# Nine of eleven feed-forward chunks: gate and up products with the weights held in the array and the tokens moving

## The chip, the cores and the metric

The kernel runs on one core of a Trainium2 chip. The metric is the device time of one launch in microseconds (us); lower is better. The core has a matrix engine (TensorE, PE in the profile, its weight loads under PEld), VectorE (DVE), ScalarE (ACT), GpSimd (POOL) and SyncE (SP), which issues the loads from the chip's memory (HBM). The engines run side by side and meet only at semaphores.

## The reference, cut to what matters

Two blocks run over 256 tokens of width 1024. The first holds four feed-forward layers (two for each of its two mixer layers), the second ends in a mixture of experts. What the change touches is the feed-forward layer, four times:

```python
def rmsnorm(x, g):
    y = x * rsqrt(mean(x * x, axis=-1) + 1e-6)      # one factor for each token
    return y * g                                    # one factor for each column
def swiglu(h, w_gate, w_up, w_down):                # 1024 -> 2816 -> 1024
    return (silu(h @ w_gate) * (h @ w_up)) @ w_down
x = x + 0.5 * swiglu(rmsnorm(x, norm), w_gate, w_up, w_down)
```

## The kernel before, in words

Weights come as pieces of 128x2048 fp32 values through a ring of three buffers. Each piece is rounded by ScalarE to the matrix engine's one-pass format (`high`, `round_piece`, L230), and VectorE takes the rest (`low = raw - high`, `split_piece`, L236). A product is then three matmuls (`product`, L241): high x high, high x low and low x high, accumulated in PSUM. Each of the three has a weight load of its own.

The hidden width of 2816 is cut into 11 chunks of 256. For a chunk there are two pieces with gate and up columns (`gate_up_parts`, each with 4 of the 8 row blocks of 128) and one piece with the rows of the down matrix. The transposed tokens `hT_high`, `hT_low` are not yet multiplied by the root factor of the norm (`rstd`); that factor is one number for each token and is applied afterwards.

`gate_up_pe` (L510) holds 128x128 of the tokens in the array and moves 512 weight columns, 256 of gate and 256 of up. The result of tile `tt` has the tokens in its partitions and stands in PSUM bank `GU[tt]`. ScalarE reads the gate half (`gate_act`, Silu with `scale=rstd`), VectorE multiplies the up half by `rstd` and by the gate (`gate_dve`), and the result `act_tok` has the tokens in its partitions. The down product needs it the other way round: `act_turn_pe` (L522) makes four 128x128 transposes into `TURN_A`, ScalarE rounds them to `aT_high` (`inner`, L635) and VectorE takes the rest into `aT_low` (L673). `down_tile` holds 128x128 of these and moves 512 columns of the down piece.

The order on the matrix engine in `ffn_pe`, for `chunk(c, m)`: first half of the gate and up products of chunk m+1 (24 matmuls), the transposes of chunk m, the second half of chunk m+1 (24), the down products of chunk m (24). `chunk(0, 0)` stands alone, eight more turns are a loop (`pe.Fori(0, N_CHUNKS - 3)`), and the last two chunks are written out, since they are woven with the start of the next norm. ScalarE and VectorE have loops of the same length with their own order: round/split of a piece, the gate work, round/split, `inner`, round/split. Each layer so has 11 sets of transposes, one for each chunk.

Names and lines to follow: `used` counts the pieces that the matrix engine is done with, `gu_first` the first bank of a chunk's gate and up products, `act_ready` the finished `act_tok` tiles, `a_low` the finished `aT_low`, `split` the pieces ready to be multiplied.

Of the kernel before, what the change touches and what calls it, by code (L numbers as in the profile page):

```python
# [28 lines left out]
F32 = mybir.dt.float32  # L29
# [7 lines left out]
P = 128  # L37
# [57 lines left out]
def build(nc, t, out):  # L95
    ctx = ExitStack()
    with ctx:
        def sb(name, shape, dt=F32):
            return ctx.enter_context(nc.sbuf_tensor(name, shape, dt))

        def sem(name):
            return ctx.enter_context(nc.semaphore(name))
# [15 lines left out]
        gate = sb("gate", [P, TT, CHUNK])  # L118
        act_tok = sb("act_tok", [P, TT, CHUNK])
# [64 lines left out]
        a_turned, a_high, a_low = sem("a_turned"), sem("a_high"), sem("a_low")  # L184
        in_first, in_copied = sem("in_first"), [sem("in_copied0"), sem("in_copied1")]
# [26 lines left out]
        def scales_with(r, n):  # L212

            return 0 if isinstance(r, int) and r == 0 else r * n
# [333 lines left out]
        AS = N_CHUNKS + 1  # L548

        def ffn_pe(pe, i, k, k_next):  # L550
# [37 lines left out]
            for tt in range(TT):  # L588
                pe.wait_ge(act_ready, 2 * (m + done) + tt + 1)
                gate_up_pe(pe, at + 2, 0, tt)  # L590
            act_turn_pe(pe, 2 * (m + done + 1))
# [5 lines left out]
            act_turn_pe(pe, 2 * (m + done + 2), (0,))  # L597
# [8 lines left out]
            act_turn_pe(pe, 2 * (m + done + 2), (1,))  # L606
# [23 lines left out]
        def ffn_act(act, i, k, k_next, aside=lambda: None):  # L630
# [10 lines left out]
            def chunk(p, r, number, a_number, gu_used):  # L641
                round_piece(act, p, r)
                gate_act(act, 0, gu_first, number)
                gate_act(act, 1, used, gu_used)
                round_piece(act, p + 1, r)
                inner(a_number)
                round_piece(act, p + 2, r)

            have_rstd(act, k)
            chunk(b + 2, 0, done + 1, a_done + 1, b + 2)  # L650
            with act.Fori(0, N_CHUNKS - 3) as c:
                chunk(b + 5, c, c + (done + 2), c + (a_done + 2), c * 3 + (b + 4))
            aside()
            m = N_CHUNKS - 2
            at = b + 3 * m
            round_piece(act, at + 2)
            gate_act(act, 0, gu_first, done + m + 1)
            gate_act(act, 1, used, at + 1)
            round_piece(act, at + 3)
            round_piece(act, at + 4)  # L660
            inner(a_done + m + 1)
            round_piece(act, at + 5)
            gate_act(act, 0, gu_first, done + m + 2)
            inner_of(0, a_done + m + 2)
            gate_act(act, 1, used, at + 4)
            tail_act(act, k_next, at + 6, at + 7, lambda: inner_of(1, a_done + m + 3))

        def ffn_dve(dve, i, k, k_next, aside=lambda: None):
# [11 lines left out]
            def chunk(p, r, number, a_number):  # L680
                split_piece(dve, p, r)
                for tt in range(TT):
                    gate_dve(dve, number * 2, tt)
                split_piece(dve, p + 1, r)
                inner(a_number)
                split_piece(dve, p + 2, r)

            have_rstd(dve, k)
            chunk(b + 2, 0, done + 1, a_done + 1)
            with dve.Fori(0, N_CHUNKS - 3) as c:  # L690
                chunk(b + 5, c, c + (done + 2), c + (a_done + 2))
            aside()
            m = N_CHUNKS - 2
            at = b + 3 * m
            split_piece(dve, at + 2)
            for tt in range(TT):
                gate_dve(dve, (done + m + 1) * 2, tt)
            split_piece(dve, at + 3)
            split_piece(dve, at + 4)
            inner(a_done + m + 1)  # L700
            gate_dve(dve, (done + m + 2) * 2, 0)
            split_piece(dve, at + 5)
            inner_of(0, a_done + m + 2)
            gate_dve(dve, (done + m + 2) * 2, 1)
            tail_dve(dve, k_next, at + 6, at + 7, 0.5, lambda: inner_of(1, a_done + m + 3))
# [1621 lines left out]
```

## Time and profile before

| | value |
|---|---|
| median of 3 runs | 1688.84 us (1688.37 to 1692.07) |
| profiled execution | 1687.54 us, its span 1685.5 us |
| PE busy | 1466.4 us, 87% of the span |
| PEld busy | 1124.0 us, 67% |
| DVE busy | 751.7 us, 45% |
| ACT busy | 615.4 us, 37% |
| mean granted TensorE clock | 0.938 of full |

The span is the time from the first to the last instruction of the profiled execution; some 2 us lie around it. "Busy" of PE counts overlapped matmuls once. A view with groups of instructions gives the mean length of one; since matmuls are pipelined, the length of one (0.39 us) is more than the distance from one start to the next (0.23 us), and only the distance tells what one costs in a stream.

### The profile page before, as it was taken

What the parts mean: (1) busy time and instruction counts of PE and PEld (TensorE: products, weight loads), DVE (VectorE), ACT (ScalarE), POOL (GpSimd) and SP (SyncE); (2) the same over time, 40 slices, a digit from 0 to 9 for tenths busy, and PEclk for the clock granted to TensorE, in tenths of its full rate; (3) what the DMA queues carried; (4) which work ended last, traced back from release to release, by engine and by line L of the source; (5) the groups of instructions that cost most, each with busy time, mean ns of one, the idle gap of its engine ahead of it and who ended that gap; (6) DMA issues with size and microseconds to landing.
All of it is one profiled execution on the core that took longest, in us unless ns stands there. A gap on an engine that the chain in (4) does not pass through costs nothing.

```text
span 1685.5 us, 22438 instructions
## 1 busy us (share of the span) xinstructions
PE 1466.4 (87%) x8732; PEld 1124.0 (67%) x8732; DVE 751.7 (45%) x985; ACT 615.4 (37%) x783; POOL 34.3 (2%) x66
## 2 busy tenths in 40 slices
PE   7999998699999999999999999966587666766766
PEld 5888887588888888877788887855554434424434
DVE  4454648755455545465454546645521120221121
ACT  5343545354434534466553445643210110111010
POOL 4000000000000000000010000010000000000000
PEclk9999989899999999999999999987797888888978
DMA  7646544035555555553365554542599999999997
GB/s 215 218 158 216 184 166 175 1 125 201 173 202 172 184 191 185 206 164 118 125 199 180 197 176 153 197 124 102 212 418 418 418 417 417 418 419 418 418 417 315
DMA packets 172620, 396.56 MB, mean 235 GB/s; under 512 B 11361, under 2 KB 109745, under 8 KB 156192
## 3 DMA queue, kind: packets, MB, share of 16 engines
q1 hardware_dynamic: 169152, 392.20, 62.4%
q0 software_dynamic: 3296, 3.73, 1.1%
q8 instruction: 28, 0.46, 0.1%
q14 instruction: 16, 0.13, 0.0%
q10 hardware_dynamic: 128, 0.03, 0.0%
HBM read 393.83 MB, written 1.05 MB: 234 GB/s over the span
## 4 chain that ended last, share of the span: by engine, by line
PE 67%; DMA 12%; SPq 9%; DVE 7%; ACT 2%; issue 2%; POOL 0%; DVEq 0%; ACTq 0%
PE psum L243 19%; PE psum L245 18%; PE psum L244 18%; DMA pair_ring<-in_w_exp_up 9%; SPq L1945 8%; PE psum L1990 4%; PE psum L2011 2%; DMA scratch<-proj 2%; PE psum L2030 1%; DMA pair_ring<-in_w_exp_down 1%; DVE low L238 1%; PE psum L525 1%; DVE hT_low L408 1%; ACT hT_high L398 1%; PE psum L1161 1%
## 5 line engine op out<-in xcount | busy, mean ns | idle before, releaser
L238 DVE TENSOR_TENSOR low<-raw,high 128x2048 fp32r<-128x2048 f32 x179 | 406.5, 2289 | 138.7 <-ACT high L234 135.8
L243 PE MATMUL psum<-high,hT_high 128*128 128x512 f32 x1088 | 437.1, 402 | 13.9 <-DVE low L2258 5.0
L245 PE MATMUL psum<-high,hT_low 128*128 128x512 f32 x1088 | 427.9, 393 | 0.0
L244 PE MATMUL psum<-low,hT_high 128*128 128x512 f32 x1088 | 427.2, 393 | 0.0
L234 ACT ACTIVATE high<-raw 128x2048 fp32r<-128x2048 f32 x179 | 338.2, 1911 | 61.9 <-PE psum L245 53.9
L243 PEld LDWEIGHTS psum<-high,hT_high 128*128 128x128 f32 x1088 | 206.7, 190 | 59.8 <-issue 9.5
L245 PEld LDWEIGHTS psum<-high,hT_low 128*128 128x128 f32 x1088 | 206.2, 190 | 44.7
L244 PEld LDWEIGHTS psum<-low,hT_high 128*128 128x128 f32 x1088 | 207.1, 190 | 40.8
L2011 PE MATMUL psum<-pair_ring,scratch 128*32 128x256 f32 x2048 | 144.8, 435 | 55.4 <-DMA pair_ring<-in_w_exp_up 54.3
L2011 PEld LDWEIGHTS psum<-pair_ring,scratch 128*32 128x32 f32 x2048 | 68.5, 122 | 128.2 <-DMA pair_ring<-in_w_exp_up 74.3
L635 ACT ACTIVATE aT_high<-psum 128x512 fp32r<-128x512 f32 x40 | 23.9, 598 | 323.1 <-PE psum L525 323.1
L673 DVE TENSOR_TENSOR aT_low<-psum,aT_high 128x512 fp32r<-128x512 f32 x40 | 27.7, 692 | 255.3 <-ACT aT_high L635 255.3
L243 PE MATMUL psum<-high,aT_high 128*128 128x512 f32 x352 | 137.4, 390 | 0.2
L244 PE MATMUL psum<-low,aT_high 128*128 128x512 f32 x352 | 137.0, 389 | 0.0
L245 PE MATMUL psum<-high,aT_low 128*128 128x512 f32 x352 | 137.0, 389 | 0.0
L2030 PE MATMUL psum<-pair_ring,scratch 128*32 128x256 f32 x1024 | 82.4, 476 | 44.7 <-DMA pair_ring<-in_w_exp_down 40.4
L2081 ACT ACTIVATE scratch<-psum 32x256 f32<-32x256 f32 x64 | 23.9, 373 | 199.6 <-PE psum L2030 199.2
L2103 DVE TENSOR_TENSOR scratch<-scratch,psum 128x128 f32<-128x128 f32 x32 | 9.2, 288 | 188.0 <-ACT scratch L2076 188.0
L2030 PEld LDWEIGHTS psum<-pair_ring,scratch 128*32 128x32 f32 x1024 | 40.5, 130 | 72.9 <-issue 53.3
L2076 ACT ACTIVATE scratch<-psum 128x128 f32<-128x128 f32 x32 | 8.9, 278 | 210.3 <-PE psum L2011 210.3
L1990 PE MATMUL psum<-proj,h 128*128 128x128 f32 x288 | 71.1, 409 | 8.2 <-DVE proj L1898 8.2
L1990 PEld LDWEIGHTS psum<-proj,h 128*128 128x128 f32 x288 | 69.4, 335 | 13.1 <-issue 13.1
(317 smaller groups left out, 1172.7 us busy)
## 6 DMA issues: line engine op xcount, KB each, us to landing
pair_ring<-in_w_exp_gate SPq DMA_DIRECT2D x64, 1024.0 KB, 22.1
pair_ring<-in_w_exp_up SPq DMA_DIRECT2D x64, 1024.0 KB, 22.8
pair_ring<-in_w_exp_down SPq DMA_DIRECT2D x64, 1024.0 KB, 22.4
raw<-in_ffn_w_gate SPq DMA_DIRECT2D x88, 512.0 KB, 4.1
raw<-in_ffn_w_up SPq DMA_DIRECT2D x88, 512.0 KB, 5.3
raw<-in_ffn_w_down SPq DMA_DIRECT2D x88, 512.0 KB, 4.0
raw<-in_gla_w_in SPq DMA_DIRECT2D x24, 512.0 KB, 4.6
raw<-in_sb_w_in SPq DMA_DIRECT2D x24, 512.0 KB, 4.6
```

Of the source, the lines that this page charges most:

```text
L234: act.activation(high[:, p % RING, :], raw_of(p), ACT.Copy).then_inc(rounded, 1)
L238: dve.tensor_tensor(low[:, p % RING, :], raw_of(p), high[:, p % RING, :].bitcast(F32), ALU.subtract).then_inc(split, 1)
L243: pe.matmul(psum_out, lhs_high, rhs_high, start=start, stop=False, skip_group_check=True)
L244: pe.matmul(psum_out, lhs_high, rhs_low, start=False, stop=False, skip_group_check=True)
L245: return pe.matmul(psum_out, lhs_low, rhs_high, start=False, stop=stop, skip_group_check=True)
L635: act.activation(flat(aT_high), TURN_A, ACT.Copy).then_inc(a_high, 1)
L673: dve.tensor_tensor(flat(aT_low), TURN_A, flat(aT_high).bitcast(F32), ALU.subtract).then_inc(a_low, 1)
L1945: sp.dma_start(dst, src).then_inc(pair_landed[i % PAIRS], 16)
L1990: ins = pe.matmul(BATCH_X[:, k * P:(k + 1) * P], h[:, tt, :].rearrange("p (n k) -> p k n", k=KD)[:, k, :], picks[:, tt * P:(tt + 1) * P], ...
L2011: ins = pe.matmul(out_rows, batch_x[:, kk, j * SLOTS:(j + 1) * SLOTS], w[:, :, k, c * P:(c + 1) * P], start=kk == 0, stop=kk == KD - 1, sk ...
L2030: ins = pe.matmul(ITEM_Y[q * SLOTS:(q + 1) * SLOTS, :], item_aT[:, c * SLOTS:(c + 1) * SLOTS], w[:, c, q * QUARTER:(q + 1) * QUARTER], sta ...
L2081: ins = act.activation(batch_y[j * SLOTS:(j + 1) * SLOTS, q * QUARTER:(q + 1) * QUARTER], ITEM_Y[q * SLOTS:(q + 1) * SLOTS, :], ACT.Copy)
```

## The change

The gate and up products of chunks 1 to 9 of each layer change their roles. `gate_up_turned_pe` holds 128x128 of the weights in the array (one block `c` of 128 columns of gate, then of up) and moves the 256 tokens. A bank `GU[c]` so holds gate (256 columns) and up (256 columns) of 128 hidden units, with the hidden units in the partitions, as the down product wants them. A piece of half a chunk takes 2 x 4 x 2 x 3 = 48 matmuls of 256 columns in place of 24 of 512. The transposes of these chunks go away.

The root factor now varies along the columns, so a row of it is made once for each layer: two matmuls with `rstd` spread over 128 columns as the held operand and the identity as the moving one (`ROOT_ROWS`), copied to `root_rows`. VectorE multiplies each bank by it (`block_norm`, 128x512), ScalarE makes the Silu (`block_silu_act`), VectorE the product with up (`block_gate`), ScalarE the rounding (`block_high_act`) and VectorE the rest (`block_low`). Chunks 0 and 10 of each layer stay as they were. `aT_high` is written as soon as the down products of the chunk before are done.

```diff
+        def gate_up_turned_pe(pe, q, half, c):
+            for k in range(4):
+                kk = 4 * half + k
+                for i in range(2):
+                    cols = slice(i * CHUNK + c * P, i * CHUNK + (c + 1) * P)
+                    ins = product(pe, GU[c][:, i * TOKENS:(i + 1) * TOKENS], four_k(high, q)[:, k, cols],
+                                  four_k(low, q)[:, k, cols], hT_high[:, kk, :], hT_low[:, kk, :],
+                                  start=kk == 0 and i == 0, stop=kk == KD - 1)
+            if c == 1:
+                ins.then_inc(used, 1)
+            elif half == 1:
+                ins.then_inc(gu_first, 1)
...
             def chunk(c, m, start=False):
...
-                for tt in range(TT):
-                    pe.wait_ge(act_ready, scales_with(c, 2) + (2 * (m + done) + tt + 1))
-                    gate_up_pe(pe, b + at + 2, 0, tt)
-                act_turn_pe(pe, scales_with(c, 2) + 2 * (m + done + 1))
+                for n in range(2):
+                    if m == 0:
+                        pe.wait_ge(act_ready, 4 * i + n + 1)
+                    else:
+                        pe.wait_ge(block_normed, scales_with(c, 2) + (BLOCKS * i + 2 * (m - 1) + n + 1))
+                    gate_up_turned_pe(pe, b + at + 2, 0, n)
+                if m == 0:
+                    act_turn_pe(pe, 4 * i + 2)
+                    have_rstd(pe, k)
+                    for tt in range(TT):
+                        ins = pe.matmul(ROOT_ROWS[:, tt * P:(tt + 1) * P], rstd[:, tt:tt + 1].to_broadcast([P, P]),
+                                        ident[:, :], start=True, stop=True, skip_group_check=True)
+                    ins.then_inc(rows_of_roots, 1)
...
-                for tt in range(TT):
-                    gate_up_pe(pe, b + at + 3, 1, tt)
+                for n in range(2):
+                    gate_up_turned_pe(pe, b + at + 3, 1, n)
...
+            with act.Fori(0, N_CHUNKS - 3) as c:
+                number = c * 2 + (BLOCKS * i + 1)
+                round_piece(act, b + 5, c)
+                for n in range(2):
+                    block_silu_act(n, number)
+                round_piece(act, b + 6, c)
+                act.wait_ge(used, c * 3 + (b + 5))
+                for n in range(2):
+                    block_high_act(n, number)
+                round_piece(act, b + 7, c)
...
+            with dve.Fori(0, N_CHUNKS - 3) as c:
+                number = c * 2 + (BLOCKS * i + 1)
+                split_piece(dve, b + 5, c)
+                block_norm(0, gu_first, c + (done + 2), c + (a_done + 1))
+                block_norm(1, used, c * 3 + (b + 4), None)
+                for n in range(2):
+                    block_gate(n, number)
+                split_piece(dve, b + 6, c)
+                for n in range(2):
+                    block_low(n, number)
+                split_piece(dve, b + 7, c)
```

In the written-out part after the loop the transposes of chunk 9 go, and the wait ahead of the first gate and up products of chunk 10 is on `block_normed`. `gate` and `act_tok` share a new buffer `inner_sb` with the normed banks.

## Rows read from the trace of the kernel before

**Rows 1.** The page: busy time of each engine, and the chain's lines.
```profile
PE 1466.4 (87%) x8732; PEld 1124.0 (67%) x8732; DVE 751.7 (45%) x985; ACT 615.4 (37%) x783; POOL 34.3 (2%) x66
...
PE psum L243 19%; PE psum L245 18%; PE psum L244 18%; DMA pair_ring<-in_w_exp_up 9%; SPq L1945 8%; PE psum L1990 4%; PE psum L2011 2%; DMA scratch<-proj 2%; PE psum L2030 1%; DMA pair_ring<-in_w_exp_down 1%; DVE low L238 1%; PE psum L525 1%; DVE hT_low L408 1%; ACT hT_high L398 1%; PE psum L1161 1%
```
**Rows 2.** Busy time in layers 0 and 2 of four: window, length, engines (count), clock, DMA share, GB/s.
```profile
28.00:190.00 162.00, 162.00 (x728) 133.87 (x727) 80.47 (x61) 67.58 (x61) 5.90 (x9) 0.99 0.57 195
...
541.00:720.00 179.00, 178.64 (x815) 147.44 (x813) 93.40 (x83) 81.61 (x85) 0.00 (x0) 1.00 0.55 188
```
**Rows 3.** Timeline of PE, loop turns: start us, us, line, operation.
```profile
85.15 0.60 PE L525 MATMUL psum<-ident,act_tok 128*128 128x128 f32 x4
...
101.71 0.39 PE L245 MATMUL psum<-high,hT_low 128*128 128x512 f32 x1
101.95 0.60 PE L525 MATMUL psum<-ident,act_tok 128*128 128x128 f32 x4
102.30 0.48 PE L243 MATMUL psum<-high,hT_high 128*128 128x512 f32 x1
102.61 0.40 PE L244 MATMUL psum<-low,hT_high 128*128 128x512 f32 x1
...
104.70 0.39 PE L244 MATMUL psum<-low,hT_high 128*128 128x512 f32 x1
...
105.15 0.39 PE L243 MATMUL psum<-high,hT_high 128*128 128x512 f32 x1
...
118.53 0.39 PE L245 MATMUL psum<-high,hT_low 128*128 128x512 f32 x1
118.76 0.60 PE L525 MATMUL psum<-ident,act_tok 128*128 128x128 f32 x4
```
**Rows 4.** Timeline of PE: 16 moving columns, each with a full weight load.
```profile
216.51 0.26 PE L245 MATMUL psum<-gkw_high,hT_low 128*128 128x16 f32 x1
...
219.19 0.26 PE L245 MATMUL psum<-gkw_high,hT_low 128*128 128x16 f32 x1
```
**Rows 5.** Lengths ns min/median/max: the products with 16 and with 512 moving columns.
```profile
L243 PE MATMUL psum<-gkw_high,hT_high x9: 172/256/256, 216.4 to 219.0; 128*128 128x16 f32 x9
...
L245 PE MATMUL psum<-high,hT_low x3: 388/389/389, 23.8 to 25.1; 128*128 128x512 f32 x3
```
**Rows 6.** Timeline of PE: full fp32 matmuls, 128 and 256 moving columns.
```profile
301.54 2.05 PE L927 MATMUL psum<-scratch 128*128 128x128 f32 x16 [1.41 <-DVE scratch L1053]
...
318.38 2.43 PE L936 MATMUL psum<-proj,scratch 128*128 128x256 f32 x10 [1.38 <-DVE scratch L1089]
320.64 0.59 PE L939 MATMUL psum<-proj,scratch 128*128 128x256 f32 x2
```
**Rows 7.** Timeline of DVE and ACT within one loop turn, and in turn 0.
```profile
103.21 0.69 DVE L673 TENSOR_TENSOR aT_low<-psum,aT_high 128x512 fp32r<-128x512 f32 x1 [7.34 <-ACT aT_high L635]
105.02 4.49 DVE L238 TENSOR_TENSOR low<-raw,high 128x2048 fp32r<-128x2048 f32 x2 [1.11 <-ACT high L234]
109.43 0.87 DVE L618 SCALAR_TENSOR_TENSOR act_tok<-psum,rstd,gate 128x256 f32<-128x256 f32 x2
...
102.58 0.60 ACT L635 ACTIVATE aT_high<-psum 128x512 fp32r<-128x512 f32 x1 [9.04 <-PE psum L525]
103.08 3.71 ACT L234 ACTIVATE high<-raw 128x2048 fp32r<-128x2048 f32 x2
106.69 0.46 ACT L614 ACTIVATE gate<-psum,rstd 128x256 f32<-128x256 f32 x1
...
37.80 4.50 DVE L238 TENSOR_TENSOR low<-raw,high 128x2048 fp32r<-128x2048 f32 x2 [1.11 <-ACT high L234]
```
**Rows 8.** Timeline of PE among the experts: 64 matmuls in one burst.
```profile
1223.60 3.64 PE L2011 MATMUL psum<-pair_ring,scratch 128*32 128x256 f32 x64
```
**Rows 9.** Windows of PE around the 16-column products: length, busy, clock, DMA, GB/s.
```profile
216.40:219.20 2.80, 2.80 (x28) 1.00 0.63 162
219.60:223.60 4.00, 4.00 (x21) 0.50 0.96 359
```

More of the change, by code:

```diff
@@ L117, in build @@
         h = sb("h", [P, TT, D])
-        gate = sb("gate", [P, TT, CHUNK])
-        act_tok = sb("act_tok", [P, TT, CHUNK])
+        inner_sb = sb("inner_sb", [P, 2, 2 * CHUNK])
+        gate, act_tok = (inner_sb[:, i, :].rearrange("p (a n) -> p a n", a=TT) for i in range(2))
         gain = sb("gain", [P, 2, D])
@@ L184, in build @@
         a_turned, a_high, a_low = sem("a_turned"), sem("a_high"), sem("a_low")
+        rows_of_roots, roots_spread = sem("rows_of_roots"), sem("roots_spread")
+        block_normed, block_silu, block_act, block_high = (sem("block_" + n) for n in ("normed", "silu", "act", "high"))
         in_first, in_copied = sem("in_first"), [sem("in_copied0"), sem("in_copied1")]
@@ L596, in ffn_pe @@
             down_tile(pe, at + 4, 0)
-            act_turn_pe(pe, 2 * (m + done + 2), (0,))
+            act_turn_pe(pe, 4 * (i + 1), (0,))
             gate_up_pe(pe, at + 3, 1, 1)
@@ L605, in ffn_pe @@
             down_tile(pe, at + 4, 1)
-            act_turn_pe(pe, 2 * (m + done + 2), (1,))
+            act_turn_pe(pe, 4 * (i + 1), (1,))
             x_turn_pe(pe, k_next, 0)
@@ L639, in inner_of, with block_silu_act, block_high_act @@
                 act.activation(inner_tile(aT_high, tt), turned_inner(tt), ACT.Copy).then_inc(a_high, 1)
[L641 to L647, printed above, removed]
-            have_rstd(act, k)
-            chunk(b + 2, 0, done + 1, a_done + 1, b + 2)
-            with act.Fori(0, N_CHUNKS - 3) as c:
-                chunk(b + 5, c, c + (done + 2), c + (a_done + 2), c * 3 + (b + 4))
+            def block_silu_act(n, number):
+                act.wait_ge(block_normed, number + n)
+                act.activation(inner_sb[:, n, 0:TOKENS], inner_sb[:, n, 0:TOKENS], ACT.Silu).then_inc(block_silu, 1)
+            def block_high_act(n, number):
+                act.wait_ge(block_act, number + n)
+                act.activation(aT_high[:, n, :], inner_sb[:, n, 0:TOKENS], ACT.Copy).then_inc(block_high, 1)
+            have_rstd(act, k)
+            round_piece(act, b + 2)
+            gate_act(act, 0, gu_first, done + 1)
+            gate_act(act, 1, used, b + 2)
+            round_piece(act, b + 3)
+            inner(3 * i + 1)
+            round_piece(act, b + 4)
+            with act.Fori(0, N_CHUNKS - 3) as c:
+                number = c * 2 + (BLOCKS * i + 1)
[7 more added lines that the diff above has]
+                round_piece(act, b + 7, c)
             aside()
@@ L678, in inner_of, with block_norm @@
                                   ALU.subtract).then_inc(a_low, 1)
[L680 to L686, printed above, removed]
-            have_rstd(dve, k)
-            chunk(b + 2, 0, done + 1, a_done + 1)
-            with dve.Fori(0, N_CHUNKS - 3) as c:
-                chunk(b + 5, c, c + (done + 2), c + (a_done + 2))
+            def block_norm(n, counter, value, lows):
+                dve.wait_ge(counter, value)
+                if n == 0:
+                    dve.wait_ge(a_low, lows)
+                dve.tensor_tensor(inner_sb[:, n, :].rearrange("p (o n) -> p o n", o=2),
+                                  GU[n].rearrange("p (o n) -> p o n", o=2),
+                                  root_rows.rearrange("p (o n) -> p o n", o=1).to_broadcast([P, 2, TOKENS]),
+                                  ALU.mult).then_inc(block_normed, 1)
@@ new lines, in ffn_dve @@
+            have_rstd(dve, k)
+            split_piece(dve, b + 2)
+            for tt in range(TT):
+                gate_dve(dve, 4 * i + 2, tt)
+            split_piece(dve, b + 3)
+            inner(3 * i + 1)
+            dve.wait_ge(rows_of_roots, i + 1)
+            dve.tensor_copy(root_rows, ROOT_ROWS).then_inc(roots_spread, 1)
+            split_piece(dve, b + 4)
+            dve.wait_ge(roots_spread, i + 1)
+            with dve.Fori(0, N_CHUNKS - 3) as c:
+                number = c * 2 + (BLOCKS * i + 1)
+                split_piece(dve, b + 5, c)
+                block_norm(0, gu_first, c + (done + 2), c + (a_done + 1))
+                block_norm(1, used, c * 3 + (b + 4), None)
+                for n in range(2):
+                    block_gate(n, number)
+                split_piece(dve, b + 6, c)
+                for n in range(2):
+                    block_low(n, number)
+                split_piece(dve, b + 7, c)
@@ L694, in ffn_dve @@
             at = b + 3 * m
+            number = BLOCKS * (i + 1) - 1
             split_piece(dve, at + 2)
-            for tt in range(TT):
-                gate_dve(dve, (done + m + 1) * 2, tt)
+            block_norm(0, gu_first, done + m + 1, a_done + m)
+            block_norm(1, used, at + 1, None)
+            for n in range(2):
+                block_gate(n, number)
             split_piece(dve, at + 3)
+            for n in range(2):
+                block_low(n, number)
             split_piece(dve, at + 4)
-            inner(a_done + m + 1)
-            gate_dve(dve, (done + m + 2) * 2, 0)
+            gate_dve(dve, 4 * i + 4, 0)
             split_piece(dve, at + 5)
-            inner_of(0, a_done + m + 2)
-            gate_dve(dve, (done + m + 2) * 2, 1)
-            tail_dve(dve, k_next, at + 6, at + 7, 0.5, lambda: inner_of(1, a_done + m + 3))
+            inner_of(0, 3 * i + 2)
+            gate_dve(dve, 4 * i + 4, 1)
+            tail_dve(dve, k_next, at + 6, at + 7, 0.5, lambda: inner_of(1, 3 * i + 3))
         IN_ORDER = ["gla_in", "sb_in", "mix_in"]
```

27 lines of the change are left out of this document (20 added, 7 removed).

## The prediction

> **What bounds the kernel now.** I read four views. The page first: the matrix engine is busy for 87% of the span, and three lines of its products hold 55% of the chain that ended last [rows 1]. Second the windows of the feed-forward layers: TensorE is busy 162.00 of 162 us in the first and 178.64 of 179 in the third, at a granted clock of 0.99 and 1.00, while VectorE has about half of that time and ScalarE 42 to 46% [rows 2]. So in these layers nothing but the stream of matmuls sets the time. Third the timeline of one loop turn, since a stream is priced by the distance from one start to the next, not by the length of one. The transposes start at 85.15, 101.95 and 118.76, so a turn is 16.80 us [rows 3]. From the start at 105.15 to that at 118.53 there are 59 steps: 13.38 / 59 = 226.7 ns for one product matmul of 512 columns, with the seam of the loop within the stretch and invisible [rows 3]. 72 such matmuls are 16.32 us. The other 0.48 us of the turn is at the transposes: from 101.71 to 102.61 there are 0.90 us where two ordinary steps would be 0.45, and the nine steps after it (102.61 to 104.70) are 232 ns instead of 227, another 0.05 [rows 3]. Fourth the short matmuls elsewhere in the trace, for the price of the new form.
>
> **What goes.** Nine sets of four transposes in each of four layers, 36 sets. Each is on the path, with the exposed load behind it: 36 x 0.48 = 17.4 us saved. Eight sets a layer are in the loop; the ninth stands between the same two groups of products in the written-out part, so it costs the same.
>
> **What changes form.** A chunk's gate and up products are 48 x 226.7 ns = 10.88 us now and become 96 matmuls of 256 columns, each with a 128-column weight load of its own. The columns streamed are equal; the loads double. Everything hangs on p, the distance between two such matmuls. No row shows this form, so I bound it.
> - From below by the load: products with 16 moving columns and the same load run from 216.51 to 219.19 in 24 steps, 111.7 ns each [rows 4]. Full-fp32 matmuls with 128 columns, which stream as long as 256 one-pass columns would, give the same: 16 in 2.05 us, less the length of one (0.275, and 0.10 for the exposed first load), over 15 steps is 111.7 ns [rows 6]. So a load and a stream of this size do overlap, and p is at least 111.7.
> - From above by a fixed price: 512 columns at the 2.4 GHz of clock 1.00 would be 213.3 ns, the step is 226.7, so there are 13.3 ns too many. If they belong to the matmul and not to its columns, p = 106.7 + 13.3 = 120.0.
> - Between them: the 13.3 ns look like a price of columns. The first 16-column product, whose load had been done, took 172 ns; a 512-column one took 388, also with no load after it (it is the last ahead of a gap) [rows 5]. 216 ns more for 496 columns is 0.435 ns a column, where 2.4 GHz would be 0.417; the short one shows no 13 ns of its own. Also 256-column fp32 matmuls, two passes over the same 512 column times, step at (320.64 - 318.38 - 0.10) / 10 = 216 ns, so a fixed price of load and swap is some 2.5 ns [rows 6]. A cost by the column makes p = 226.7 / 2 = 113.3, just above the load's floor.
>
> I take p = 113.3: the gate and up products then cost 96 x 113.3 = 10.88 us, exactly what they do now, and the whole gain of the transposes is kept.
>
> The Trainium skill (TensorE: Matmul & The Clock Gate, Back-to-back issue gap) gives a warm gap of N / 2.4 + 2.5 ns. The fp32 row with its 216 ns agrees, the one-pass products with 226.7 don't. By that rule alone the estimate for 256 columns is 109.2 ns, below the floor that the loads show, so the measured rows decide here.
>
> **What is added on TensorE.** Two fp32 matmuls of 128 columns for the row of roots, in each layer: 8 x 111.7 ns [rows 6] = 0.9 us. They stand right behind transposes that stay, and rstd has been there since the Silu of chunk 0. The loop body grows from 76 to 120 matmuls with their loads. Issue doesn't bind: among the experts 64 matmuls with their loads ran in 3.64 us, 54 ns a pair [rows 8].
>
> **What changes on the other engines, costed at nothing.** VectorE before: three splits (two in 4.49), 0.87 for the gates, 0.69 for the rest [rows 7], about 8.3 us a turn. After: three splits 6.7, two norms of 128x512 out of PSUM at the 0.69 of L673, four operations of 128x256 between 0.35 (half of L673) and 0.48 (L618 at worst): 9.5 to 10.0 of 16.3. ScalarE: three roundings (two in 3.71), two Silus of 0.46, two roundings of 128x256 at 0.3 to 0.46: under 7.5 [rows 7]. The cover is the stream of matmuls, so dates count. Let t be the start of a loop body on TensorE. Half 0 of the next chunk's products is done at 5.4, bank 0 is whole at 8.2, bank 1 at 10.9, the down products end at 16.3. The next body's first piece is rounded once half 0 has freed its buffer (half of 3.71) and split after that (half of 4.49), until about 9.6, then norm 0 until 10.3, norm 1 from 10.9 to 11.6, Silus and gates until about 12.7; the banks are wanted again at 16.3, so 4.7 us are spare. Behind these waits on VectorE is queued the split of half 1, wanted at 21.8 and done at about 17. The new wait of ScalarE for the end of the down products (16.3) has the two roundings behind it, then the rounding and split of the down piece: all done by about 21.5, wanted at 27.2. Now the activations are ready 4.0 us before the down products want them (L673 ends at 103.90 [rows 7]; the down products start 24 matmuls after 102.30 [rows 3], at 107.9); after the change they are ready some 9 us before. Turn 0 adds a wait for the row and a copy of 128x256 (under 0.48) in a place where VectorE sits idle for 1.11 us ahead of L238 [rows 7]. SyncE's loads wait for splits as before; no queue is passed. If this cover were gone, a wait of 1 us a turn would cost 36 us.
>
> **Sum.** -17.4 + 0.0 + 0.9 = -16.5 us. Against the profiled execution (span 1685.5, 1687.5 in all) that is 1671.0; the median of the runs is 1.3 us above that execution, so 1672.3.
>
> **The rivals.**
> - *Fixed price.* The 13.3 ns are paid by every one-pass matmul, so twice as often. p = 120.0 costs 96 x 6.67 ns = 0.64 us a chunk, 23.0 in all; 1672.3 + 23.0 = 1695.3, slower than before. For it: nothing in the trace shows 256 columns, and the load now fills the whole matmul where it filled half. Against it: the lengths of rows 5 and the fp32 steps of rows 6. It turns the sign from p = 118.1 on. The same page of the Trainium skill says in that section that in a sustained stream the spacing is set by load and matmul together, 81 ns for N = 128; that speaks for a price by the load, and no run here shows that form.
> - *No settling.* After each set of transposes the steps are 232 ns for some nine matmuls before they settle at 226.7 [rows 3]. If the short form stays in the unsettled state, p = 116.1 and 96 x 2.8 ns x 36 = 9.6 us come back: 1681.9.
> - *Load floor.* If the column price is only there in long streams, p = 111.7, 96 x 1.63 ns x 36 = 5.6 us more gain: 1666.7.
> - *A chain or the clock.* A wait takes the place of the transposes (my dates are off by over 4.7 us), or the clock falls: the 16-column products ran at 1.00 for 2.8 us and then at 0.50 [rows 9]. The turned form streams as many columns in the same time as now, so I expect no fall. From 17 us of such loss, half a us a chunk, it is slower than before; about 1695 or more.
> - *It doesn't do what it says.* The transposes go for certain, and the matmul count is fixed by the code; the part that can fail is p, above.
>
> **Chances.** Forecast 0.55, load floor 0.08, no settling 0.18, fixed price 0.14, chain or clock 0.05. What this kernel's measurement can tell from no change is about 0.2%, 3.4 us, so faster means under 1685.4. Forecast, floor and nearly all of no settling are there: 0.80. The stretch of p between 117.1 and 119.1 is same: 0.05. The rest, 0.15, is slower. The range leaves out the fixed price and the chain, 0.19 together: low 1665, from the floor's 1666.7 and some run to run; high 1690, which is p = 118.4.
>
> **What would show it.** In the profile after, the turn of a layer's loop is 16.32 us with no transposes in it (16.16 at the floor, 16.6 unsettled, 16.96 at the fixed price). The start-to-start of a 256-column product is 0.113 us. L525 falls from 176 matmuls (44 sets of four) to 32. TensorE has no more idle time ahead of the products in the loops than now (none), and its clock in the layers at 1.00. The prediction is wrong if p is over 118, whatever else holds, or if a wait of TensorE for a block of VectorE shows in each turn.

## The result and the profile after

The changed kernel takes 1693.86 us (median of 19 runs, 1691.99 to 1697.42), the one before 1689.73 us beside it on the same chip (19 runs, 1687.15 to 1692.60). The ratio is 1.0028 with a 95% interval of 1.0021 to 1.0036: slower by 0.28%. The forecast was 1672.3, with a range up to 1690 and a chance of 0.8 for faster. Time and sign are both wrong. What came true is the rival called fixed price, at 1695.3.

The profiled execution after took 1693.36 us with a span of 1691.6, at a mean granted clock of 0.941. The page after: busy time of each engine, the lines of the chain, and the largest group of the new form (busy us, mean ns of one | idle before it and its releaser).
```profile
PE 1469.6 (87%) x10332; PEld 1199.1 (71%) x10332; DVE 803.0 (47%) x1097; ACT 623.3 (37%) x819; POOL 34.2 (2%) x66
...
PE psum L245 19%; PE psum L247 19%; PE psum L246 19%; DMA pair_ring<-in_w_exp_up 9%; SPq L2022 9%; PE psum L2067 4%; DMA scratch<-proj 2%; PE psum L2088 2%; PE psum L2107 1%; DMA pair_ring<-in_w_exp_down 1%; DVE low L240 1%; DVE hT_low L410 1%; ACT hT_high L400 1%; PE psum L1238 1%; ACT high L236 1%
...
L245 PE MATMUL psum<-hT_high,high 128*128 128x256 f32 x1152 | 326.4, 283 | 2.7 <-DVE inner_sb L645 2.7
```
Beside [rows 1] the chain has lost the transposes (L525, 1%), and the three lines of products hold 57% of it instead of 55%. Matmuls grew from 8732 to 10332. The idle time ahead of the 1152 new matmuls on L245 is 2.7 us in the whole kernel; on L246 and L247 it is 0.0. Of the 2.7 us 2.43 stand in the first layer, ahead of chunk 1, where the kernel before waits 1.85 us for VectorE in the same place (L618). So no wait took the place of the transposes.

The window of the third feed-forward layer after: window, length, busy (count) of PE, PEld, DVE, ACT, POOL, then clock, DMA share, GB/s.
```profile
551.00:730.00 179.00, 178.75 (x1202) 165.49 (x1201) 102.54 (x103) 80.68 (x85) 0.00 (x0) 1.00 0.57 188
```
TensorE is as full as in [rows 2], at the same clock, with half as many matmuls again in 179 us. Nothing but the stream sets the time here, before and after, so the time is in the stream's steps.

The timeline of PE over one loop turn after: start us, length us, line, operation.
```profile
92.16 0.40 PE L245 MATMUL psum<-high,aT_high 128*128 128x512 f32 x1
...
109.02 0.28 PE L247 MATMUL psum<-hT_high,low 128*128 128x256 f32 x1
109.14 0.40 PE L245 MATMUL psum<-high,aT_high 128*128 128x512 f32 x1
109.37 0.40 PE L246 MATMUL psum<-low,aT_high 128*128 128x512 f32 x1
...
114.38 0.39 PE L247 MATMUL psum<-high,aT_low 128*128 128x512 f32 x1
114.60 0.28 PE L245 MATMUL psum<-hT_high,high 128*128 128x256 f32 x1
114.72 0.28 PE L246 MATMUL psum<-hT_low,high 128*128 128x256 f32 x1
...
118.20 0.28 PE L245 MATMUL psum<-hT_high,high 128*128 128x256 f32 x1
```
A turn is 109.14 - 92.16 = 16.98 us, where it was 16.80 [rows 3]. From 114.72 to 118.20 there are 29 steps: 3.48 / 29 = 120.0 ns for one product of 256 columns. The forecast had 113.3. The 24 down products of a turn start at 109.14 and the turned ones at 114.60: 5.46 / 24 = 227.5 ns, of which the first five, behind the change from 256 to 512 columns, take 228 to 236 ns each; before, all 24 step at 226.7. That is 0.02 us more a turn. So a turn's 0.18 us are 0.64 for the longer stream of gate and up products and 0.02 here, less the 0.48 of the transposes. Nine chunks of 0.18 us and about half a us for the row of roots make 2 us a layer. The transposes of `x` on either side of the third layer show it: they came at 540.7 and 728.4, 187.7 us apart, and come at 543.8 and 733.3, 189.5 apart.

### The profile page after: what moved, and what is told of

It is laid out like the page before. It is cut to its first block, busy times and chain, and to the rows that moved or that the text cites. A ratio compares the mean times of both kernels' runs of the same rounds, so it can differ in the third digit from the quotient of the medians.

```text
span 1691.6 us, 25942 instructions
## 1 busy us (share of the span) xinstructions
PE 1469.6 (87%) x10332; PEld 1199.1 (71%) x10332; DVE 803.0 (47%) x1097; ACT 623.3 (37%) x819; POOL 34.2 (2%) x66
## 4 chain that ended last, share of the span: by engine, by line
PE 67%; DMA 12%; SPq 9%; DVE 6%; ACT 3%; issue 2%; POOL 0%; DVEq 0%; ACTq 0%
PE psum L245 19%; PE psum L247 19%; PE psum L246 19%; DMA pair_ring<-in_w_exp_up 9%; SPq L2022 9%; PE psum L2067 4%; DMA scratch<-proj 2%; PE psum L2088 2%; PE psum L2107 1%; DMA pair_ring<-in_w_exp_down 1%; DVE low L240 1%; DVE hT_low L410 1%; ACT hT_high L400 1%; PE psum L1238 1%; ACT high L236 1%
## 5 line engine op out<-in xcount | busy, mean ns | idle before, releaser
L245 PE MATMUL psum<-hT_high,high 128*128 128x256 f32 x1152 | 326.4, 283 | 2.7 <-DVE inner_sb L645 2.7
L247 PE MATMUL psum<-hT_high,low 128*128 128x256 f32 x1152 | 326.0, 283 | 0.0
L246 PE MATMUL psum<-hT_low,high 128*128 128x256 f32 x1152 | 326.0, 283 | 0.0
L245 PEld LDWEIGHTS psum<-hT_high,high 128*128 128x128 f32 x1152 | 221.0, 192 | 4.7 <-DVE low L240 3.2
L246 PEld LDWEIGHTS psum<-hT_low,high 128*128 128x128 f32 x1152 | 221.0, 192 | 1.3
L247 PEld LDWEIGHTS psum<-hT_high,low 128*128 128x128 f32 x1152 | 221.0, 192 | 0.0
L245 PE MATMUL psum<-high,hT_high 128*128 128x512 f32 x512 | 208.2, 407 | 12.2 <-DVE low L2335 5.0
L247 PE MATMUL psum<-high,hT_low 128*128 128x512 f32 x512 | 203.0, 396 | 0.0
L246 PE MATMUL psum<-low,hT_high 128*128 128x512 f32 x512 | 202.6, 396 | 0.0
L245 PE MATMUL psum<-high,aT_high 128*128 128x512 f32 x352 | 137.8, 392 | 0.2
L246 PE MATMUL psum<-low,aT_high 128*128 128x512 f32 x352 | 137.4, 390 | 0.0
L247 PE MATMUL psum<-high,aT_low 128*128 128x512 f32 x352 | 137.0, 389 | 0.0
L245 PEld LDWEIGHTS psum<-high,hT_high 128*128 128x128 f32 x512 | 98.1, 192 | 35.7 <-issue 9.3
L247 PEld LDWEIGHTS psum<-high,hT_low 128*128 128x128 f32 x512 | 98.1, 192 | 21.5
L246 PEld LDWEIGHTS psum<-low,hT_high 128*128 128x128 f32 x512 | 98.4, 192 | 19.1
L2180 DVE TENSOR_TENSOR scratch<-scratch,psum 128x128 f32<-128x128 f32 x32 | 9.2, 287 | 189.5 <-ACT scratch L2153 189.5
L2158 ACT ACTIVATE scratch<-psum 32x256 f32<-32x256 f32 x64 | 23.9, 373 | 200.5 <-PE psum L2107 200.1
```

The lines of the kernel that those rows point to most:

```text
L245: pe.matmul(psum_out, lhs_high, rhs_high, start=start, stop=False, skip_group_check=True)
L246: pe.matmul(psum_out, lhs_high, rhs_low, start=False, stop=False, skip_group_check=True)
L247: return pe.matmul(psum_out, lhs_low, rhs_high, start=False, stop=stop, skip_group_check=True)
L2158: ins = act.activation(batch_y[j * SLOTS:(j + 1) * SLOTS, q * QUARTER:(q + 1) * QUARTER], ITEM_Y[q * SLOTS:(q + 1) * SLOTS, :], ACT.Copy)
```

## The experiments

Each kernel ran beside the kernel before on the same chip. In the texts on record F is the fixed price of each one-pass fp32 matmul, C a price by the column, L a price that goes with the length of the weight load, and G a rounding of the step up to multiples of 13.3 ns.

**The step by itself, over lengths and types.** Behind the last stage of the kernel before, TensorE runs streams of matmuls, each with a 128-column weight load of its own, with nothing else at work. The 138 us that this adds mean nothing; the starts do.
```diff
             moe_pe(pe)
+            pe.wait_ge(micro_go, 2)
...
+            def stream(n, count, start=False, dsts=(4,), src=(hi, lo), width=P, shift=1):
+                for i in range(count):
+                    at = shift * (i % 3)
+                    w = src[0][:, at * P:at * P + width]
+                    m = src[i % 2][:, at * 512:at * 512 + n]
+                    pe.matmul(banks(dsts[i % len(dsts)])[0:width, 0:n], w, m, start=start or i < len(dsts), stop=True,
+                              skip_group_check=True)
+            stream(512, 64)
+            for n in (512, 448, 384, 320, 256, 192, 128, 64):
+                stream(n, 32)
...
+            stream(256, 32, start=True)
...
+            stream(256, 32, dsts=(4, 5))
...
+            full = (hi.bitcast(F32), lo.bitcast(F32))
+            stream(256, 32, src=full)
+            stream(128, 32, src=full)
+            half = ones[:, :].bitcast(mybir.dt.bfloat16)
+            for n in (512, 256):
+                stream(n, 32, src=(half, half), shift=0)
+            for width in (64, 32):
+                stream(512, 32, width=width)
```


> The kernel before, with streams of matmuls on TensorE behind its last stage, each matmul with its own weight load; the kernel's result is not touched, its time is longer by the streams. It measures the start-to-start of one-pass products by the number of moving columns N, in streams of 32. Theory F (a fixed price of 13.3 ns for each one-pass matmul): N = 512, 448, 384, 320, 256 step at N/2.4 + 13.3 = 226.7, 200.0, 173.3, 146.7, 120.0 ns, and from N = 192 down the weight load sets the step, at 111.7. Theory C (a price by the column, 0.443 ns each, and 120.0 at N = 256 from load and stream getting in each other's way): 226.7, 198.3, 170.0, 141.7, and 120 for 256 and below. Theory L (the price belongs to the weight load): with only 64 or 32 columns held, 512 moving columns step at 220.0 or 216.7; F says 226.7 with any load. Further streams tell where the price hangs: clearing in place of accumulating, and two PSUM banks in turn, change nothing by F; full fp32 with 256 and 128 columns, accumulating, steps at 216 and 111.7 if the price belongs to the one-pass form, and above 220 if it belongs to accumulation; bfloat16 with 512 and 256 columns steps at 216 and 109 if the price belongs to reading four bytes a column at full rate.

Measured: windows of PE, each from the first start of a stream to the first start of the next: length, busy (count, which takes in a neighbour or two), clock, DMA share, GB/s. In order: one-pass products with 448, 384, 320, 256 and 192 columns; full fp32 with 256 and 128; bfloat16 with 512; one-pass with 512 columns against 64 and 32 held ones.
```profile
1705.54:1712.02 6.48, 6.48 (x33) 1.00 0.01 3
1712.02:1717.60 5.58, 5.58 (x34) 1.00 0.00 0
1717.60:1722.28 4.68, 4.68 (x33) 1.00 0.00 0
1722.28:1726.12 3.84, 3.84 (x35) 1.00 0.00 0
1726.12:1729.67 3.55, 3.55 (x34) 1.00 0.02 5
1773.62:1787.43 13.81, 13.81 (x65) 1.00 0.00 0
1787.43:1794.57 7.14, 7.14 (x65) 1.00 0.01 2
1794.79:1801.48 6.69, 6.69 (x31) 1.00 0.00 0
1804.90:1812.33 7.43, 7.43 (x35) 1.00 0.00 0
1812.34:1819.74 7.40, 7.40 (x33) 1.00 0.01 2
```
The one-pass streams have 32 matmuls, so the lengths divide by 32: 202.5, 174.4, 146.3, 120.0 and 110.9 ns. The first steps of a stream are not yet settled (the first of all is 91 ns at 192 columns, which makes that mean too short). Read from start to start within the settled part of each stream, against the column time at 2.4 GHz:

| columns | step, ns | columns / 2.4 GHz | left over |
|---|---|---|---|
| 512 | 226.7 | 213.3 | 13.3 |
| 448 | 202.5 | 186.7 | 15.8 |
| 384 | 173.3 | 160.0 | 13.3 |
| 320 | 146.7 | 133.3 | 13.3 |
| 256 | 120.0 | 106.7 | 13.3 |
| 192, 128, 64 | 111.6, 111.7, 111.7 | 80.0, 53.3, 26.7 | no longer falls |

The same 13.3 ns stand behind 512, 384, 320 and 256 columns: a price of the matmul and not of its columns. C wanted 198.3, 170.0 and 141.7 ns for 448, 384 and 320 columns, 3 to 5 ns less than each took, and falls. `start=True` on each matmul and two banks in turn leave 120.0 and 226.7 as they are, so it is no price of accumulation or of the bank. With 64 or 32 held columns the step is 7.43 / 32 = 232 and 7.40 / 32 = 231 ns: a shorter load takes nothing off, and L, which wanted 220.0 or 216.7, falls. F wanted 226.7 here as well; the 230.0 and 231.7 ns of the settled parts are 3 to 5 more, and no run shows why.

The other types don't pay it. Full fp32 leaves two records for each matmul, 64 in a stream: 13.81 / 64 = 215.8 and 7.14 / 64 = 111.6 ns. The first is 512 column times and 2.5 ns if each record stands for two passes over its 256 columns, as the prediction took it. Bfloat16 with 512 columns has 31 records, 6.69 / 31 = 215.8 ns, and with 256 columns 109.2 ns from start to start. So the price belongs to the one-pass fp32 form. The full fp32 streams read the same operands as the one-pass ones; the bfloat16 streams read another tile, at one address throughout, so by themselves they would not tell type from operands.

The Trainium skill (TensorE: Matmul & The Clock Gate, Back-to-back issue gap) gives N / 2.4 + 2.5 ns for an isolated warm gap, 215.8 and 109.2; the bfloat16 streams agree to the tenth and the one-pass fp32 ones don't, at 226.7 and 120.0. For a sustained stream of loads and matmuls the same section gives 131 ns at N = 512; no stream here came near it, and the measurement decides.

**Without the transposes.** The 36 sets of transposes go; the down products then read the activations of chunk 0 of their layer, so this part isn't computed. Roundings of the activations wait for the end of the first half's products instead.
```diff
-                act_turn_pe(pe, scales_with(c, 2) + 2 * (m + done + 1))
+                if m == 0:
+                    act_turn_pe(pe, 2 * (done + 1))
...
-            act_turn_pe(pe, 2 * (m + done + 1))
...
-                act.wait_ge(a_turned, number)
+                act.wait_ge(counter, number)
```


> The kernel before, with the transposes of chunks 1 to 9 left out in each layer (36 sets of four); the down products of these chunks then use stale activations, so that part of the computation is wrong in value and the same in amount. It measures the gain side of the change alone. If the 0.48 us that I read at each set are its price: a loop turn of 16.32 us and 17.4 us less in all, near 1672. The rival, that a large part of this is only moved (a wait for the rounding of the activations takes its place): a turn stays over 16.5 us and less than 10 us are gained.

Measured: 1670.22 us (4 runs) against 1689.08 (15 runs), ratio 0.9889 [0.9874, 0.9904]. The profiled span is 1668.1 against 1685.5, 17.4 us less; the medians differ by 18.9, and the interval, 16 to 21 us, holds both. The timeline of PE of this kernel, from the first down product of one turn to that of the next:
```profile
73.01 0.39 PE L243 MATMUL psum<-high,aT_high 128*128 128x512 f32 x1
...
89.10 0.39 PE L245 MATMUL psum<-high,hT_low 128*128 128x512 f32 x1
89.33 0.39 PE L243 MATMUL psum<-high,aT_high 128*128 128x512 f32 x1
```
The turn is 89.33 - 73.01 = 16.32 us, 72 steps of 226.7 ns. The gain of this term was sized right, 36 x 0.48, and it arrives in full at the end. It is the bound for any way of getting rid of the transposes.

**The joined products.** If each matmul pays the same, fewer and longer ones should give the gain back. The piece `high` of the weights is held for two products, with `hT_high` and with `hT_low`; with the two side by side in SBUF one matmul of 512 columns does both, its halves of the bank added by VectorE at the end. 96 matmuls a chunk become 32 of 512 and 32 of 256. Otherwise this is the changed kernel; chunk 1 keeps the changed form.
```diff
+        hT_both = sb("hT_both", [P, 2, KD, TOKENS], F32R)
...
+        def gate_up_wide_pe(pe, q, half, c):
+            for k in range(4):
+                kk = 4 * half + k
+                for i in range(2):
+                    cols = slice(i * CHUNK + c * P, i * CHUNK + (c + 1) * P)
+                    pe.matmul(wide_bank(c, i), four_k(high, q)[:, k, cols], hT_both[:, :, kk, :], start=kk == 0, stop=False,
+                              skip_group_check=True)
+                    ins = pe.matmul(wide_bank(c, i)[:, 0:TOKENS], four_k(low, q)[:, k, cols], hT_high[:, kk, :], start=False,
+                                    stop=kk == KD - 1, skip_group_check=True)
...
```


> The changed kernel, where for chunks 2 to 9 the two matmuls that hold the same rounded weights (against the high and the low part of the tokens) are one matmul of 512 columns into a bank of its own, so 64 matmuls a chunk in place of 96 (32 of 512 and 32 of 256 columns); VectorE adds the two halves of a bank, two more operations of 128x512 for each block. The columns streamed are the same. By a fixed price for each matmul, a chunk's products fall from 11.52 to 32 x (226.7 + 120.0) ns = 11.09 us, the loop turn from 16.98 to 16.55, and 32 chunks give back 13.7 us: about 1680, faster than both kernels. By a price of the column or of load against stream that 256-column matmuls alone pay, the 512-column ones among them would not settle and less than 8 us come back. If VectorE's four more operations of some 0.65 us a turn come late, a wait for the normed blocks shows ahead of each turn and the gain is lost.

Measured: 1689.44 us (11 runs) against 1689.08 (15 runs), ratio 1.0 [0.9991, 1.001]: no faster, where about 1680 was expected. The span is 1687.7. The timeline of PE of this kernel, within the joined products and at the start of the down products of two turns:
```profile
103.24 0.40 PE L547 MATMUL psum<-hT_both,high 128*128 128x512 f32 x1
103.48 0.28 PE L549 MATMUL psum<-hT_both,low 128*128 128x256 f32 x1
103.60 0.40 PE L547 MATMUL psum<-hT_both,high 128*128 128x512 f32 x1
103.83 0.28 PE L549 MATMUL psum<-hT_both,low 128*128 128x256 f32 x1
103.95 0.40 PE L547 MATMUL psum<-hT_both,high 128*128 128x512 f32 x1
104.18 0.28 PE L549 MATMUL psum<-hT_both,low 128*128 128x256 f32 x1
104.30 0.40 PE L547 MATMUL psum<-hT_both,high 128*128 128x512 f32 x1
...
109.60 0.40 PE L246 MATMUL psum<-high,aT_high 128*128 128x512 f32 x1
...
126.39 0.40 PE L246 MATMUL psum<-high,aT_high 128*128 128x512 f32 x1
```
The turn is 16.79 us, not the 16.55 expected. TensorE never waits for the longer work of VectorE (a copy, an addition and a product of 128x512 at 0.68 to 0.69 us each). The loss is in the pairs: three of them, from 103.24 to 104.30, take 1.06 us, 353.3 ns a pair, where one step of each length would be 226.7 + 120.0 = 346.7. 32 pairs with 6.6 ns too many are 0.21 us a turn, most of the 0.24 that were missed; the down products behind them take some hundredths more than settled steps would. Going back and forth between the lengths costs something that long streams of one length don't pay.

**Lengths between, and mixtures.** Two questions in the manner of the first experiment: is the step rounded up to multiples of 13.3 ns (G), and what does the change of length cost?
```diff
+            for n in (504, 496, 488, 480, 464, 288, 280, 272, 264, 248, 240):
+                stream(n, 32)
+                stream(512, 16)
+            def groups(size, count):
+                for r in range(count):
+                    stream(512, size)
+                    stream(256, size)
+            groups(1, 16)
...
+            groups(8, 4)
...
+            groups(16, 2)
...
+            groups(32, 1)
```


> As the first run with streams: the kernel before, then streams of one-pass matmuls with a weight load each. First streams of 32 with N = 504, 496, 488, 480, 464, 288, 280, 272, 264, 248 and 240 columns, each followed by 16 of 512. The settled steps so far (226.7, 173.3, 146.7, 120.0 ns for 512, 384, 320, 256) are whole multiples of 13.33 ns. Theory F (a fixed price of 13.3): 504 steps at 223.3, 496 at 220.0, 488 at 216.7, 480 at 213.3, 280 at 130.0, 264 at 123.3, 248 at 116.7. Theory G (the step is N/2.4 + 2.5 rounded up to the next multiple of 13.33 ns): 504, 496 and 488 all at 213.3, 480 at 213.3, 280, 272 and 264 at 120.0, 288 at 133.3, 248 at 120.0. Then mixtures of 512 and 256 columns: one by one (32 matmuls), in groups of 8 (64), of 16 (64) and of 32 (64). A one-by-one pair took 353 ns in the kernel with joined matmuls, against 346.7 for the sum of the settled steps. If each change of length costs a few steps until the stream settles, pairs cost 353 one by one, about 349 in groups of 8, 348 in groups of 16; if the loss is there for any mixture, 353 in all.

Measured: windows of PE as above. In order: 504, 496 and 264 columns; then mixtures of 512 and 256 columns, 16 pairs one by one, and 32 pairs in groups of 8, of 16 and of 32.
```profile
1698.24:1705.49 7.25, 7.25 (x33) 1.00 0.00 0
1709.14:1716.18 7.04, 7.04 (x33) 1.00 0.00 0
1774.91:1778.75 3.84, 3.84 (x33) 1.00 0.00 0
1796.92:1802.56 5.64, 5.64 (x33) 1.00 0.01 3
1806.22:1817.36 11.14, 11.14 (x65) 1.00 0.00 0
1821.02:1832.12 11.10, 11.10 (x65) 1.00 0.01 1
1835.78:1846.86 11.08, 11.08 (x65) 1.00 0.00 0
```
504 columns step at 7.25 / 32 = 226.6 ns and 496 at 220.0, where G wants 213.3 for both. G falls. F puts 504 at 223.3, 496 at 220.0 and 264 at 123.3 (measured 120.0); over the eleven lengths the measured means lie between 3.3 ns under F and 9 over it. 504 columns cost as much as 512. At many of the lengths between, the steps don't settle but swing: between 217 and 242 ns at 488 columns, where the 9 is, 212 and 221 at 480, 205 and 215 at 464, 117 and 123 at 264, 109 and 119 at 248. So the fixed price holds to a few ns and is no exact law. A pair costs 352.5 ns one by one and 348.1, 346.9 and 346.3 ns in groups of 8, 16 and 32. Within the groups the first five steps after the change to 512 columns are 228 to 236 ns, and then 226.7.

**Joined products, grouped.** The same joined matmuls, sixteen of 512 columns first and then sixteen of 256 in each half of a chunk.
```diff
+            blocks = [(c, k, i) for c in range(2) for k in range(4) for i in range(2)]
+            for c, k, i in blocks:
+                cols = slice(i * CHUNK + c * P, i * CHUNK + (c + 1) * P)
+                pe.matmul(wide_bank(c, i), four_k(high, q)[:, k, cols], hT_both[:, :, 4 * half + k, :],
+                          start=half == 0 and k == 0, stop=False, skip_group_check=True)
+            for c, k, i in blocks:
+                cols = slice(i * CHUNK + c * P, i * CHUNK + (c + 1) * P)
+                ins = pe.matmul(wide_bank(c, i)[:, 0:TOKENS], four_k(low, q)[:, k, cols], hT_high[:, 4 * half + k, :],
+                                start=False, stop=half == 1 and k == 3, skip_group_check=True)
...
```


> The kernel with joined matmuls, where each half of a chunk first runs its sixteen 512-column matmuls and then its sixteen 256-column ones, in place of one of each in turn. Same matmuls, same columns. If the 6.6 ns that a pair took beyond the settled steps come from the changes of length, the products of a chunk fall from 11.31 to about 11.14 us, the turn from 16.75 to about 16.6, and 5 us come back: near 1684, faster than the kernel before by some 0.3%. If the settled steps don't return in groups of 16, the time stays at that of the kernel with joined matmuls, the same as before. The first bank of a chunk is whole only 1.9 us before the second (it was 2.8), which VectorE's dates should bear.

Measured: 1682.47 us (6 runs, 1681.12 to 1683.98) against 1690.94 (11 runs), ratio 0.9953 [0.9938, 0.9967]; near 1684 was expected. It is faster than the kernel before by 0.47%, and so faster than the changed one. The timeline of PE over one turn of this kernel:
```profile
91.05 0.40 PE L246 MATMUL psum<-high,aT_high 128*128 128x512 f32 x1
...
96.52 3.79 PE L546 MATMUL psum<-hT_both,high 128*128 128x512 f32 x16
100.15 2.08 PE L550 MATMUL psum<-hT_both,low 128*128 128x256 f32 x16
...
107.63 0.40 PE L246 MATMUL psum<-high,aT_high 128*128 128x512 f32 x1
```
Sixteen steps of 512 columns take 100.15 - 96.52 = 3.63 us, 226.9 ns each. The turn is 16.58 us; its 32 joined and 24 down products at 226.7 ns and its 32 short ones at 120.0 would be 16.53. Only the order of the matmuls differs from the kernel with joined products, and 0.21 us a turn came from it.

## Why the prediction was wrong

Step by step, in the order of the prediction:

- **What bounds the kernel: right.** TensorE is busy for 178.75 of 179 us after [rows 2], the clock there is 1.00, and its idle time ahead of the new products is 2.7 us in all.
- **What goes, -17.4 us: right.** The kernel without the transposes has a turn of 16.32 and a span 17.4 us shorter.
- **What changes form, 0.0 us: wrong, and this is the step that failed.** The three bounds around p were 111.7, 113.3 and 120.0. I took 113.3, "a cost by the column", and the traces say 120.0. With 36 chunks of 96 matmuls and 6.67 ns each that is +23.0 us, which turns -17.4 into a loss.
- **The row of roots, +0.9 us: mis-sized.** A full fp32 matmul leaves two records, and each takes a step. The groups of PE after, by form, have sixteen where I counted eight:
```profile
L586 PE MATMUL psum<-ident,rstd 128*128 128x128 f32 x16 | 2.4, 275 | 0.0
```
  16 x 111.7 ns = 1.8 us. [rows 6] had shown it already, with x16 on one line; I divided that burst by its records and then counted my own by instructions.
- **The other engines at nothing: right.** The timelines of DVE and ACT in the turn whose down products run from 109.14 to 114.60 (start us, length us, line, operation, idle before):
```profile
109.34 0.69 DVE L728 TENSOR_TENSOR inner_sb<-psum,square 128x512 f32<-128x512 f32 x1 [0.92 <-PE psum L247]
109.95 0.41 DVE L735 TENSOR_TENSOR inner_sb<-inner_sb 128x256 f32<-128x256 f32 x1
115.25 0.76 DVE L740 TENSOR_TENSOR aT_low<-inner_sb,aT_high 128x256 fp32r<-128x256 f32 x2 [0.64 <-ACT aT_high L674]
...
110.06 0.42 ACT L670 ACTIVATE inner_sb<-inner_sb 128x256 f32<-128x256 f32 x1 [1.20 <-DVE inner_sb L728]
114.80 0.72 ACT L674 ACTIVATE aT_high<-inner_sb 128x256 fp32r<-128x256 f32 x2 [2.52 <-PE psum L247]
```
  The norms take 0.69 and the gates 0.41 us, as costed. The rest `aT_low` is ready at 116.01 and wanted by the next down products at 126.1, the 10 us of slack that I gave as 9. VectorE has 803.0 us instead of 751.7 [rows 1], all of it beside the stream.
- **The clock: no fall from the change, right.** In the third layer it is 1.00 before [rows 2] and after. It differs in a stretch of the first layer, and not by the change. The windows 28 to 40 us of PE, after:
```profile
28.00:40.00 12.00, 11.24 (x94) 1.00 0.58 176
```
  and of the kernel before; then of the first run with streams and of the second, which are the kernel before up to 1680 us:
```profile
28.00:40.00 12.00, 12.00 (x50) 0.86 0.56 176
28.00:40.00 12.00, 10.67 (x49) 1.00 0.56 176
28.00:40.00 12.00, 11.64 (x46) 0.86 0.56 176
```
  A clock of 0.86 means that a part of the stretch ran at the lower level of 1.2 GHz. It came in two of three executions of the same code, and so it goes with the execution. It came in the joined products too (0.86) and stayed away in the grouped ones and in the kernel without transposes (1.00 each).

The sum made again: -17.4 + 23.0 + 1.8 + 0.7 = +8.1 us, the last being the 0.02 us on 36 sets of down products, or 2.0 us a layer. The traces have it: from the transposes of `x` ahead of a layer to those at its end the second, third and fourth layers grew by 2.0, 1.9 and 2.0 us. At the end of the first the changed kernel was 1.5 us late (202.0 against 200.5), and the mixer layer behind it gave 0.4 of that back. At the last down products it was 6.9 us late (1047.7 against 1040.9), and at the end of the span 6.1.

The medians differ by 4.1 us, with an interval of 3.5 to 6.1, so by less than the layers lost. A part is the pair of executions: the one profiled before, at 1687.54, lies 2.2 us below the median of its 19 runs, and the one after within 0.5 of its own. The profiled layers themselves hardly vary: the kernel before and both runs with streams reach the last transposes of `x` in the fourth layer at 1040.0, 1039.9 and 1040.0 us. Why the 19 runs of one kernel spread over 5 us, and how the changed kernel gets back 2 to 3 us by the medians, stays open; no kept trace shows it.

**Why I chose wrongly.** Two rows were read for more than they carry. First the lengths of [rows 5]: 388 ns less 172 is 216 for 496 columns, 0.435 ns a column, and I concluded that the extra 13 ns grow with the columns. But a matmul's end is modelled in these profiles, and a length is no step. Nor do the 16 and the 512 columns lie on one line with the lengths between: the page after has 283 ns for 256 columns and 389 for 512 (L247), 0.414 a column, and in that there is no price by the column. The same trace gave the starts of only one length in the settled one-pass form, and one length can't part a slope from a constant. A 256-column one-pass product has a recorded length of 283 ns on the page after and a step of 120.0. Second the full fp32 steps of [rows 6], which show no fixed price: true, and 215.8 in the streams too, but it is another form, and the price is one of the form. The bounds were right and the true value stood on one of them. What was wrong was to place 0.14 on that end because two rows that do not hold the form spoke against it.

**The other rivals.** No settling gave p = 116.1 and is not what happened: the 29 steps in the fence above are 120.0 on average. But steps that need time to settle are real, and in the joined products they cost 0.21 us a turn. The load floor is real as well, 111.6 to 111.7 ns, and lies below the step of 256 columns by 8 ns, so it does not bind. A chain of the other engines did not form.

**What stays open.** Why a one-pass fp32 matmul pays about 13.3 ns and bfloat16 and full fp32 don't was not found, only that it does not go with the columns, the held columns, the bank or the accumulation. One thing more stands in the traces: at the lower clock it is not there. The windows of PE in the kernel before, six steps of 512 columns, and in the kernel with joined products, fourteen of 256 (its chunk 1, which keeps the changed form):
```profile
28.46:31.02 2.56, 2.56 (x8) 0.50 0.92 292
30.22:33.21 2.99, 2.99 (x16) 0.50 0.96 311
```
They step at 2.56 / 6 = 426.7 and 2.99 / 14 = 213.6 ns, which is the column time at 1.2 GHz (426.7 and 213.3) with nothing left over. A price of a fixed number of the array's clock cycles would be 26.7 ns there, and it is not seen at all. Nor was it found why some lengths and alternating lengths step unevenly.

## What to carry to other kernels

A turned product that halves the moving columns doubles the number of matmuls, so price one matmul as a constant plus its columns, from starts of at least two lengths in the same form; if the trace holds only one length, the two readings of that row are two cases of nearly equal weight, and a stream of a few microseconds tells them apart. Where the form has a constant, transposes are cheap in comparison: here 0.48 us a chunk against 48 more matmuls at 13.3 ns, 0.64 us. The gain lies in fewer and longer matmuls that hold the same weights against several moving pieces, with equal lengths in groups and not in turn.

## What the hardware showed that was not expected

- At a granted clock of 1.00 a one-pass fp32 matmul with its weight load steps at columns / 2.4 GHz plus about 13.3 ns (226.7, 173.3, 146.7 and 120.0 ns for 512, 384, 320 and 256 columns); full fp32 and bfloat16 step at 215.8 ns for 512 column times.
- From 240 columns down the step no longer falls: 111.6 to 111.7 ns at 240, 192, 128 and 64, each with a load of 128 rows and 128 columns. That the load sets it is argued; no stream gave these lengths a shorter load. With 64 or 32 held columns, 512 moving ones step at 230.0 to 231.7 ns, no faster than with 128.
- After a change from 256 to 512 columns the first five steps take 228 to 236 ns. Alternating the two costs 352.5 to 353.3 ns a pair, groups of 16 cost 346.9.
- At a granted clock of 0.50 the one-pass products step at the bare column time, 426.7 ns for 512 columns and 213.6 for 256; the 13.3 ns were seen at 1.00 alone.
- The clock of 28 to 40 us was 1.00 or 0.86 in different executions of the same code.
